# Four widths instead of three for the gate-and-up products of a mixture-of-experts visit

## The reference, cut to what matters

```python
def moe(h, w_router, b_router, w_gate_up, b_gate_up, w_down, b_down):
    xf = h.reshape(-1, D)
    logits = xf @ w_router + b_router
    top_logit, top_e = lax.top_k(logits, TOP_K)          # 4 of 32
    gates = jax.nn.softmax(top_logit, axis=-1)
    ...
    hu = lax.ragged_dot(xs, w_gate_up, group_sizes) + b_gate_up[e_sorted]
    gate = jnp.minimum(hu[:, :D_FF], SWIGLU_LIMIT)
    up = jnp.clip(hu[:, D_FF:], -SWIGLU_LIMIT, SWIGLU_LIMIT)
    act = (up + 1.0) * gate * jax.nn.sigmoid(SWIGLU_ALPHA * gate)
    y = lax.ragged_dot(act, w_down, group_sizes) + b_down[e_sorted]
    ...
```

## Time and profile before

| | |
|---|---|
| median of 3 runs | 5346.77 us (5340.24 to 5354.88) |
| the profiled execution | 5348.82 us |
| its span, from the first to the last instruction | 5347.2 us |
| PE busy | 4898.8 us, 92% of the span |
| DVE busy | 3068.7 us, 57% |
| ACT busy | 1842.8 us, 34% |
| visits | 2352 to 5052 us of the span |
| granted TensorE clock, mean | 0.959 of full speed |

### The profile page before, as it was taken

The page is one execution under the profiler, slowest core; times in us unless marked ns, Lnnn a source line. Parts: engine busy times, 40 slices in busy tenths (PEclk is TensorE's granted clock), DMA queues, the critical chain, the costliest instruction groups (busy, mean ns, idle before and its releaser), DMA issues. The chain is left out here.

```text
span 5347.2 us, 68611 instructions
## 1 busy us (share of the span) xinstructions
PE 4898.8 (92%) x23758; PEld 3552.4 (66%) x23759; DVE 3068.7 (57%) x4877; ACT 1842.8 (34%) x2663; POOL 980.4 (18%) x1073
## 2 busy tenths in 40 slices
PE   7999688899999995849999999999999999999977
PEld 3444333344444443448999999999999999999822
DVE  2222167778777778155555655565576556755522
ACT  1111123233333332224343444343454444543400
POOL 0000122111111111121211121121122112211155
PEclk9999789999999997869999999999999999999988
DMA  4332210101000000045454554465565455654355
GB/s 181 114 114 106 78 26 17 22 17 22 13 13 13 12 11 8 8 156 190 165 201 152 204 191 169 146 216 169 183 222 186 169 196 183 223 188 165 133 197 185
DMA packets 426731, 663.73 MB, mean 124 GB/s; under 512 B 22064, under 2 KB 286256, under 8 KB 425552
## 3 DMA queue, kind: packets, MB, share of 16 engines
q1 hardware_dynamic: 367776, 507.46, 29.1%
q0 software_dynamic: 26576, 85.56, 4.5%
q10 hardware_dynamic: 32256, 69.22, 3.4%
HBM read 542.86 MB, written 119.31 MB: 124 GB/s over the span
## 5 line engine op out<-in xcount | busy, mean ns | idle before, releaser
L1352 PE MATMUL gu<-x_hi,w_hi 128*128 128x256 f32 (+2 forms) x4096 | 1230.8, 300 | 1.3 <-DVE x_lo L1434 1.3
L1353 PE MATMUL gu<-x_lo,w_hi 128*128 128x256 f32 (+2 forms) x4096 | 1231.2, 301 | 0.0
L1354 PE MATMUL gu<-x_hi,w_lo 128*128 128x256 f32 (+2 forms) x4096 | 1229.0, 300 | 0.0
L1429 DVE TENSOR_TENSOR w_lo<-w_raw,w_hi 128x2048 fp32r<-128x2048 f32 x386 | 874.4, 2286 | 532.7 <-ACT w_hi L1503 532.7
L1503 ACT ACTIVATE w_hi<-w_raw 128x2048 fp32r<-128x2048 f32 x386 | 727.0, 1907 | 283.0 <-PE gu L1354 196.0
L1352 PEld LDWEIGHTS gu<-x_hi,w_hi 128*128 128x128 f32 x4096 | 772.1, 189 | 2.5 <-issue 1.7
L1354 PEld LDWEIGHTS gu<-x_hi,w_lo 128*128 128x128 f32 x4096 | 772.6, 189 | 0.0
L1353 PEld LDWEIGHTS gu<-x_lo,w_hi 128*128 128x128 f32 x4096 | 770.2, 188 | 0.7
L1325 POOL TENSOR_TENSOR a_lo<-up,a_hi 128x384 fp32r<-128x384 f32 x256 | 396.9, 1550 | 1489.4 <-ACT a_hi L1515 1489.4
L1352 PE MATMUL yp<-w_hi,a_hi 128*128 128x512 f32 x1296 | 526.0, 406 | 0.0
L1353 PE MATMUL yp<-w_lo,a_hi 128*128 128x512 f32 x1296 | 514.8, 397 | 0.0
(11 more groups left out here) (256 smaller groups left out, 5898.9 us busy)
## 6 DMA issues: line engine op xcount, KB each, us to landing
w_raw<-w_gate_up SPq DMA_DIRECT2D x258, 1024.0 KB, 7.6
w_raw<-w_down SPq DMA_DIRECT2D x128, 1024.0 KB, 6.4
y_dram<-y_rows ACTq DMA_DIRECT2D x192, 256.0 KB, 3.1
y_dram<-zeros SPq DMA_DIRECT2D x16, 2016.0 KB
h_blk<-h_dram SPq DMA_DIRECT2D x32, 512.0 KB, 6.1
qi_dram<-qi_stage ACTq DMA_DIRECT2D x16, 640.0 KB, 2.9
w_in_sb<-w_in SPq DMA_DIRECT2D x1, 8480.0 KB, 23.9
x_in<-x SPq DMA_DIRECT2D x16, 512.0 KB, 9.2
```

The costliest lines, as they stand in the source:

```text
L1352: nc.tensor.matmul(out, s_hi_, m_hi, start=(n == 0), stop=False)
L1353: nc.tensor.matmul(out, s_hi_, m_lo, start=False, stop=False)
L1354: op = nc.tensor.matmul(out, s_lo_, m_hi, start=False, stop=(n == len(pairs) - 1))
L1429: nc.vector.tensor_tensor(w_lo[:, c % 2, cols], raw[:, c % 3, cols], w_hi[:, c % 2, cols].bitcast(F32), ALU.subtract).then_inc(s_lo, 1)
```

## The change

The list of widths becomes 240, 272, 304 and 384. The kind is now a sum of three comparisons, 0 to 3. Whether the third tile of rows is computed hung on kind 0 before. It now hangs on an entry of its own in `meta` (column 3): more than 256 rows. So which visits skip the third tile stays as it was. TensorE reads two entries for each visit, and `up` stands four times in the code in place of three, in the written-out visit and in the loop.

```diff
-WIDTHS = (2 * P, 2 * P + 64, ROWS)
+WIDTHS = (2 * P - 16, 2 * P + 16, 2 * P + 48, ROWS)
...
                 nc.vector.tensor_scalar(start[:], left[:], float(WIDTHS[0]), None, ALU.is_gt)
-                nc.vector.tensor_scalar(nth[:], left[:], float(WIDTHS[1]), None, ALU.is_gt)
-                dve.drain()
-                nc.vector.tensor_tensor(S["meta"][:, :, 2], start[:], nth[:], ALU.add)
+                dve.drain()
+                for width in WIDTHS[1:-1]:
+                    nc.vector.scalar_tensor_tensor(start[:], left[:], float(width), start[:], ALU.is_gt, ALU.add)
+                    dve.drain()
+                nc.vector.tensor_copy(S["meta"][:, :, 2], start[:])
+                nc.vector.tensor_scalar(S["meta"][:, :, 3], left[:], float(2 * P), None, ALU.is_gt)
...
                 def body(v):
-                    kind = look_up(pe, v, 2, 2)
+                    kind = look_up(pe, v, 2, len(WIDTHS) - 1)
+                    third = look_up(pe, v, 3, 1)
                     pe.wait_ge(s_xl, 8 * v + 8)
...
-                                with pe.If(kind != 0):
+                                with pe.If(third != 0):
```

## The result

The changed kernel takes 5962.31 us (median of 4 runs, 5957.76 to 5969.95) against 5344.09 us for the kernel before, in the runs made beside it. The ratio is 1.1155 (95% interval 1.1134 to 1.1176): 618 us slower. I had forecast 5283 us with a range up to 5670, so the change went the other way than forecast, and the time lies outside the range.

What follows compares the result with a forecast made beforehand. PE's products were taken to bound each visit. Widths (-42.2 and -30.7), code on the way (+8.5) and `place_stage` (+0.8) summed to -63.6 us from 5348.8; with the median 2.0 us lower, the forecast was 5283 us, range 5262 to 5670.

Steps and rivals of the forecast that it cites:

- the forecast's case: Whole kernel: a clean gain from narrower up products, 5283 us, own range 5268 to 5305; chance 0.40.
- the first rival: Loop over visits: code no longer stays on the chip and is refetched every visit, net +243 us, 5590 us; chance 0.33.
- The sum: Whole kernel: widths, code on the way and `place_stage` together, -42.2 - 30.7 + 8.5 + 0.8 = -63.6 us.
- one packet too many may hide behind the queued down products: Loop over visits, argument against refetch costs: if just one packet must share its place, its fetch may be hidden.
- The price of the rival: Each loop visit: 6.86 us gap plus 3.0 us lost speed, 9.9 us, times 31, or 307 us.
- a second miss: Each loop visit, if extra code misses twice: 12.2 us a visit, 378 us in all, up to 5661 us.
- Widths above 256: Up products at 272, 304 and 384 columns, by the experts' row counts: together -42.2 us.
- Width 240: Up products of the twelve experts with at most 240 rows: -2.56 us each, -30.7 us, ends -34.8 and 0.
- neither rival about it: Up products at 240 columns: no cheaper than 256, about 5314 us (0.12), or far dearer, near 6650 us (0.10).
- The floor I looked for: Narrow up products: something other than columns may hold a product at 120 ns; plain float32 records start 106 ns apart.
- The cover by DVE: Up phase at 240 columns: DVE still waits 0.8 us for PE in each quarter, so nothing is given back, 0.
- The idle time of the first two visits: Behind the up products: jumps past more code add 5.1 and 3.4 us, +8.5 us; ends 0 and 17 us.

Runs made afterwards that it cites:

- e6: Kernel before, with 84 waits on a passed semaphore (41 instructions) run once ahead of the first visit: 5608.41 us, ratio 1.0487.
- e5: Changed kernel, with 164 waits on a passed semaphore run once ahead of the first visit: 5502.92 us, ratio 1.0273 to the kernel before.
- e9: Kernel before, with each down tile making one product of three: 5106.89 us, ratio 0.9548 to the kernel before.
- e8: Changed kernel with its four widths, each down tile making one product of three: 5043.7 us, ratio 0.9426 to the kernel before.
- e4: Kernel before, with 218 waits on a passed semaphore (108 instructions) run once ahead of the first visit: 5364.3 us, ratio 1.0003.

## Why the prediction was wrong

**The step that failed is the choice between the forecast's case and the first rival.** The sum has no term for code fetched again in the later passes of the loop, and that term measured 673 us. The rival named the place (the loop's code no longer stays on the chip), its sign in the profile (packets in every visit, gaps with "issue", a lower clock) and the loop's growth by a quarter. I gave it 0.33 and put the clean gain at 0.40, because the trace did not show what PE can hold. What I set against it, that one packet too many may hide behind the queued down products, did not hold. The loop touches nine blocks, and with one ahead they make ten; ten packets a visit were fetched in the mean, so little of the loop outlived a pass. It was far more than the one packet that I had thought of.

The Trainium skill (page "Runtime: NRT & Kernel Launch", section "Instruction fetch mechanics") has the capacity, 2048 instructions in blocks of 256, and calls the store a FIFO. The capacity agrees with the runs: in e6 the eight blocks of the loop stay, and one more upsets them. The FIFO is not borne out by all of them: the ten packets a visit of the changed kernel and the nine of e6 fit it, the two a visit of e5 do not. By that page's capacity nine blocks could not stay; I had worked out the nine blocks from it and still left the rival at one chance in three.

**The price of the rival was mis-sized.** I took one gap and its lost clock from the second visit, 9.9 us, times 31, or 12.2 us with a second miss. Measured: the loss against the sum without fetches, 5956.2 - (5347.2 - 63.6) = 673 us of span, 22 us for each of the 31 visits. 570 us of idle less 28.6 us in the first two visits is 541 us, 18 us in each of the 30 later ones, and the rest of the loss, about 130 us, comes with the clock of 0.91. The second visit of the kernel before was the wrong model: it came with the code at the loop's head already on the chip, ran the first copy and jumped over two. In the changed kernel a visit meets missing code at its head, on its way to its own copy and on the way out. A widest visit waits up to 21.1 us ahead of its products, since three copies lie before its own. So the range, whose upper end of 5670 rested on 12.2 us a visit, was too narrow even for the rival that it was meant to reach.

**What was right.** Widths above 256: 304 columns at 53.77 us (53.76 forecast), 272 at 48.23 (48.64). Width 240: 43.52 us, on the line, and neither rival about it came true. The floor I looked for is close, though, since 212 columns cost 42.86. The sum of all: -63.6 forecast, -63 between e9 and e8, both with shortened down products. That the two agree to within 1 us is in part luck, since the four runs of e9 alone spread over 29 us. The cover by DVE held. The idle time of the first two visits grew from 17.1 to 28.6 us, which is +11.5 where I had +8.5.

**What stays open.** A whole kernel with four widths in a loop of seven blocks was not tried. It would need some 160 instructions less. Nor do the runs show by what rule a block makes room for another.

## What to carry to other kernels

When a change adds code to a loop, count the loop's instructions and the blocks that they touch, with the one behind the last: here a loop of TensorE that touched seven blocks of 256 instructions was free, one that touched eight paid in some passes (e6) or a little in all (e5), and one that touched nine paid 22 us in every pass. A loop of nearly seven can fall off that edge through 41 instructions added ahead of it. The packets on the instruction queue show at once which side a kernel is on: about one for each block of the program, or several for each pass. A copy of code for a rare case is paid for by all cases; here three well chosen widths, 240, 304 and 384, saved 24 us where four cost 618.

## What the runs showed of the hardware that I had not expected

- The place of an unchanged loop in the program alone was worth 4.9% (e6), and moving the changed kernel's loop by 81 instructions won back 460 of its 618 us (e5).
- The block fetched ahead of the last counts against the capacity (e6 at eight blocks and 213 packets, e4 at seven and 60), and in e6 only behind a visit that computed its third tile: 17 visits hit, 13 not.
- Code that is missing costs clock as well as time: the granted clock was 0.91 in the visits.
- A float32r product's time does not fall with every column: 300 columns take 140.0 ns as 304 do, and 212 take 111.6 ns where 240 take 113.3.
